# A hybrid decoder step on one core: projection pieces, output tiles and paired state products in the mixer's heads

## The chip, the cores and the metric

The kernel runs on one core of a Trainium2 chip. Its engines have their own instruction streams and meet at semaphores: TensorE (PE, with its weight loads shown apart as PEld), VectorE (DVE), ScalarE (ACT), GpSimd (POOL) and SyncE (SP), which issues most of the DMAs. The metric is the device time of one execution in microseconds (us). Three executions of the kernel before took 1274.74, 1276.26 and 1278.26 us, median 1276.26.

## The reference

One decoder layer in float32 for a prompt of 512 tokens and for 8 samples of 8 tokens each (64 rows, with a state from the past). Both go through a mixer and then through a mixture of 64 experts. This is the mixer, cut to what matters here:

```python
z = einsum('bld,de->ble', h, w_in)                 # one projection of 1024 to 4104 columns
# mLSTM heads (4), per chunk of 128 tokens (a sample is one chunk of 8)
s   = einsum('bihd,bjhd->bijh', q, k) * w_intra
num = einsum('bijh,bjhe->bihe', s, v) + w_inter * einsum('bihd,bhde->bihe', q, C)
C_new = w_old * C + einsum('bjh,bjhd,bjhe->bhde', w_k, k, v)
# retention heads (4): q and k rotated, fixed decays instead of gates
y = einsum('bhij,bjhe->bihe', scores, v) + inter * einsum('bihd,bhde->bihe', q, S)
S_new = exp(L * log_g) * S + einsum('jh,bjhd,bjhe->bhde', k_w, k, v)
out = concat([head_norm(h_m) * sigmoid(mo), head_norm(y_r) * silu(rg)])
x = x + gt1 * rms_norm(out @ w_out)                # then the experts
```

The states C and S are 128 x 128 for each head and each sample; the kernel keeps the mLSTM normaliser as a 129th column of C.

## The kernel before, in words

The instructions of each engine are written by hand in one order per engine; semaphores (`S["..."]`) tie them together, and no scheduler moves anything. Every float32 matmul of the program is two MATMUL records of the trace, each with a weight load; a transpose is one.

**Projection.** The 1024 x 4104 weights come in eight blocks of 512 columns (2 MB each) through a ring of two slots. The first blocks (mLSTM v, q, k) are multiplied in one go before the heads. The other five (`mo`, `rq`, `rk`, `rv`, `rg`) are cut into halves of a unit, each of 8 steps (one step is one matmul over 128 of the 1024 input channels; 128 x 288 out for a channel unit, up to 128 x 256 for an `rv` unit, whose halves are columns). Their 336 steps are the filling of the heads: `fill(filled(h, p))` on TensorE works off steps up to a count that a table gives for head h and phase p. The halves alternate between banks 6 and 7, and ScalarE copies them out (`evac_halves`).

**Heads.** Eight heads follow each other (h = 0 to 3 mLSTM, 4 to 7 retention). On TensorE a head is: `chunks(h)`, four chunks of 128 tokens, each with two or three products and, from chunk 1 on, a wait for `nchunk` (VectorE has added the state of the chunk before); the scores and the key transposes of head h+1 stand in chunks 1 and 2; a fill ends each chunk. Then `samples(h)`: one product inside the samples and eight with their states (`q8`, 64 columns of which 8 are not zero, one sample each, added up in bank 5). Then `out_T(h-1)`, the transposes of the normed head before; `head_a(h+1)`, which opens the next head and waits for `ynT_ready` (VectorE has gated those transposes); and `deltas(h)`: eight products of 64 key rows, masked to one sample (`kw8`), with the values, in three groups of banks. VectorE adds them to the states (`sdu` counts it), then makes the masked scores of the next head (`stm`), and `chunks(h+1)` waits for both.

VectorE also rotates rq and rk (`rotate`, eight pieces of four instructions) and does the head norm in two parts, `norm_a` (statistics) and `norm_b`.

**Loads.** SP runs its DMAs in order: the states of the retention heads (`stS`, 2 MB) go into ring slot 0 when `rv` is done; the first half of w_out (`woA`, 2 MB) into ring slot 1 when the last projection half is done. GpSimd's queue stores the states when the last head's `sdu` is complete, waits for that store, and then loads `bcB`, the modulation rows of the expert input, into the place of `stS`.

**After the heads.** `y_mm(t)` multiplies output tile t (128 tokens; tile 4 the 64 sample rows) by w_out: 16 matmuls of 128 x 512, two banks. `y_mm(t)` from t = 2 waits for `x1_done` of tile t-2. VectorE then makes the residual row (`x1_done`) and the expert input (`h2_ready`, needs `bcB`), one tile after the other.

Of the kernel before, what the change touches and what calls it, by code (L numbers as in the profile page):

```python
# [9 lines left out]
ALU = mybir.AluOpType  # L10
# [101 lines left out]
def build(nc, A, O, K):  # L112

    ctx = ExitStack()
    with ctx:
# [245 lines left out]
        HALVES = 2 * (NU - UM)  # L361
        PHASES = 7
        BEFORE = 2 * 2 * HS
        SHARE = [64, 64, 56, 56, 22, 21, 21, 0]
        assert BEFORE + sum(SHARE) == HALVES * HS

        def filled(h, p):

            return BEFORE + sum(SHARE[:h]) + SHARE[h] * (p + 1) // PHASES

        def units_done(u):

            return u if u <= UM else UM + 2 * (u - UM)
# [350 lines left out]
        def _(act):  # L724
# [87 lines left out]
            def evac_halves(steps):  # L812

                nonlocal evacuated
                while evacuated < steps // HS:
                    g = evacuated
                    u, hf = UM + g // 2, g % 2
                    kind, nm, bi, c = UNITS[u]
                    bank = ps[6 + hf]
# [4 lines left out]
                    if kind == "tok":  # L824
# [14 lines left out]
            def head_c(h):  # L839
# [15 lines left out]
                evac_halves(filled(h, 4))  # L855
# [9 lines left out]
            for h in range(2 * H):  # L865
                head_c(h)
                if h + 1 < 2 * H:
                    head_a(h + 1)
                evac_halves(filled(h, 6))
# [95 lines left out]
        def _(pe):  # L965
# [88 lines left out]
            def fill(steps):  # L1054

                nonlocal stepped
                while stepped < steps:
                    g, k = stepped // HS, stepped % HS
                    kind, nm, bi, c = UNITS[UM + g // 2]
                    hf, w, bank = g % 2, ring[:, bi % 2, :].rearrange("p (c f) -> p c f", c=KC), ps[6 + g % 2]  # L1060
# [3 lines left out]
                    if kind == "tok":  # L1064
# [8 lines left out]
                    stepped += 1  # L1073

            def chunks(h):
# [9 lines left out]
                for c in range(NCH):  # L1085
# [12 lines left out]
                    fill(filled(h, c))  # L1098

            def samples(h):  # L1100
# [10 lines left out]
                for b in range(NB):  # L1111
                    st = stC[:, b, h, 0:w] if h < H else stS[:, b, h - H, :]
                    i = mm(ps[5][0:NS, 0:w], q8[:, b, :], st, start=b == 0, stop=b == NB - 1)  # L1113
# [3 lines left out]
            def deltas(h):  # L1117
# [3 lines left out]
                for bk, b0, b1 in DGROUPS:  # L1121
                    if b0 == 6:
                        fill(filled(h, 6))
                        pe.wait_ge(S["sdu"], h * NB + 3)
                    for b in range(b0, b1):
                        mm(ps[bk][:, (b - b0) * (DH + 1):(b - b0) * (DH + 1) + w], kw8[:, b, :], vv[0:NS, NCH, h, 0:w],
                           start=True, stop=True).then_inc(S["sdb"], 1)
# [59 lines left out]
            for h in range(2 * H):  # L1187
# [5 lines left out]
                if h == H:  # L1193
# [8 lines left out]
            def wo(k):  # L1202
                return woA[:, k, :] if k < H else woB0[:, k - H, :] if k < H + H // 2 else woB1[:, k - H - H // 2, :]

            def y_mm(t, heads=range(2 * H)):

                n = ROWS[t]
                if t >= 2:
                    pe.wait_ge(S["x1_done"], t - 1)
                if t == NCH:  # L1210
                    for k in heads:
                        for hf in range(2):
                            i = mm(y_half(t, hf), yT(k)[:, t * P:t * P + n],
                                   wo(k)[:, hf * 512:(hf + 1) * 512], start=k == 0, stop=k == 2 * H - 1)
                else:
                    for hf in range(2):
                        for k in heads:
                            i = mm(y_half(t, hf), yT(k)[:, t * P:t * P + n],  # L1218
                                   wo(k)[:, hf * 512:(hf + 1) * 512], start=k == 0, stop=k == 2 * H - 1)
                if heads[-1] == 2 * H - 1:  # L1220
                    i.then_inc(S["y_mm"], 1)
# [942 lines left out]
```

## Time and profile before

| | us |
|---|---|
| median of 3 executions | 1276.26 |
| profiled execution, device time | 1274.83 |
| its span in the trace | 1272.2 |
| TensorE busy in the span | 1164.1 (92%) |
| granted TensorE clock, mean | 0.962 |

The heads run from 200.73 us (first chunk product) to 471.31 us (first output tile), the output tiles to 537 us, the experts from about 588 us to the end. A row of the timeline is a run of like instructions, with its start, its length from the first start to the last end, and in brackets the idle time ahead of it and the instruction whose end released it. "PEclk" is the granted TensorE clock as a share of full speed (2.4 GHz), averaged over a stretch; an instruction runs at full or at half.

### The profile page before, as it was taken

To read this page: it belongs to the slowest core of one execution; us is meant where nothing else is said; L and a number is where in the kernel's file an instruction comes from. 1 tells how busy PE (TensorE), PEld (TensorE's weight loads), DVE (VectorE), ACT (ScalarE), POOL (GpSimd) and SP (SyncE) were. 2 spreads that over 40 slices of the span, in tenths; PEclk is the share of its full clock that TensorE was granted. 3 is DMA by queue.
4 is the path that set the end of the run, shared out by engine and by line. 5 is a ranking of instruction groups with operands and counts; after the bars stand their busy time and mean duration, and the time that the engine had idled before them with its cause. 6 is when DMAs were issued, how large, how long until landed. Compare 5 with 4: busy or idle time off the path is not lost.

```text
span 1272.2 us, 17204 instructions
## 1 busy us (share of the span) xinstructions
PE 1164.1 (92%) x6487; PEld 615.8 (48%) x6487; DVE 467.8 (37%) x1275; ACT 239.0 (19%) x517; POOL 150.4 (12%) x180
## 2 busy tenths in 40 slices
PE   2899999998898979998999999999999999999795
PEld 0435777767676754475434443434344344343232
DVE  0203551335533453574223623232232232232147
ACT  2302322221212211320111111111111111111111
POOL 5100000000010010011110211111111111111100
PEclk7999999999898989999999999999999999999868
DMA  9989231230116026184879899999999999999796
GB/s 277 324 284 309 69 54 25 58 66 18 50 52 231 1 110 221 82 316 147 341 311 414 330 395 419 417 420 403 383 419 368 407 420 382 414 398 374 259 375 264
DMA packets 75270, 337.26 MB, mean 265 GB/s; under 512 B 12250, under 2 KB 21182, under 8 KB 46126
## 3 DMA queue, kind: packets, MB, share of 16 engines
q1 hardware_dynamic: 56398, 287.25, 60.1%
q0 software_dynamic: 18784, 48.85, 10.5%
q8 instruction: 53, 0.87, 0.3%
q14 instruction: 35, 0.29, 0.1%
HBM read 312.45 MB, written 37.24 MB: 275 GB/s over the span
## 4 chain that ended last, share of the span: by engine, by line
PE 82%; DMA 8%; DVE 6%; issue 2%; ACT 1%; SPq 1%; POOLq 0%; DVEq 0%; POOL 0%; ACTq 0%
PE bank L1373 26%; PE bank L1397 13%; PE bank L1069 9%; PE bank L1218 4%; DMA mem<-in_w_ada 3%; PE bank L1361 3%; PE bank L1153 3%; PE bank L1066 3%; PE bank L1160 3%; PE bank L1161 2%; PE bank L1476 2%; DMA mem<-in_w_exp_down 2%; DMA mem<-expert_out_rows 2%; PE bank L997 1%; PE bank L1113 1%
## 5 line engine op out<-in xcount | busy, mean ns | idle before, releaser
L1373 PE MATMUL bank<-mem 128*32 128x512 f32 (+2 forms) x1424 | 307.0, 596 | 3.9 <-issue 3.0
L1373 PEld LDWEIGHTS bank<-mem 128*32 128x32 f32 (+2 forms) x1424 | 101.2, 127 | 162.3 <-issue 160.8
L1397 PE MATMUL bank<-mem 128*32 128x512 f32 (+2 forms) x712 | 157.0, 596 | 2.3 <-DMA mem<-in_w_exp_down 1.3
L1985 DVE COPY mem<-bank 128x512 f32<-128x512 f32 x49 | 33.9, 692 | 306.9 <-PE bank L1361 306.9
L1373 PE MATMUL bank<-x_sb,mem 128*32 128x512 f32 (+2 forms) x480 | 141.4, 594 | 1.2 <-issue 1.2
L1069 PE MATMUL bank<-hT,mem 128*128 128x288 f32 x512 | 135.5, 416 | 1.0 <-ACT mem L793 1.0
L1069 PEld LDWEIGHTS bank<-hT,mem 128*128 128x128 f32 x512 | 96.3, 195 | 26.7 <-issue 2.4
L925 ACT ACTIVATE mem<-bank 128x256 f32<-128x256 f32 x48 | 18.5, 385 | 322.7 <-PE bank L1383 322.7
L1397 PEld LDWEIGHTS bank<-mem 128*32 128x32 f32 (+2 forms) x712 | 48.8, 126 | 58.9 <-issue 58.0
L1397 PE MATMUL bank<-hT,mem 128*32 128x512 f32 (+2 forms) x240 | 72.8, 596 | 0.8 <-ACT mem L925 0.8
L1373 PEld LDWEIGHTS bank<-x_sb,mem 128*32 128x32 f32 (+2 forms) x480 | 43.6, 127 | 59.8 <-issue 59.8
L678 POOL DMA_INDIRECT mem<-ffn_in_rows,idxg x34 | 35.2, 1034 | 295.4 <-DVE idxs L1981 255.4
L2000 DVE COPY hT<-bank 128x512 f32<-128x512 f32 x48 | 33.2, 692 | 86.9 <-PE bank L1397 86.8
L694 POOL DMA_INDIRECT expert_out_rows<-hT,idxs x48 | 48.6, 1013 | 108.0 <-DVE hT L2000 99.3
L1218 PE MATMUL bank<-mem 128*128 128x512 f32 x128 | 55.6, 594 | 1.0 <-DVE mem L1745 1.0
L931 ACT ACTIVATE hT<-bank 128x512 f32<-128x512 f32 x48 | 28.7, 597 | 143.2 <-PE bank L1397 143.2
L997 PE MATMUL bank<-mem 128*32 128x512 f32 x192 | 27.0, 675 | 20.4 <-DMA mem<-in_w_ada 20.4
L1476 PE MATMUL bank<-mem,c_ident 128*128 128x512 f32 (+1 forms) x72 | 40.8, 729 | 3.8 <-DMA mem<-expert_out_rows 3.8
L1943 DVE SCALAR_TENSOR_TENSOR mem<-mem,c_iota 128x160 bf16<-128x160 f32 (+3 forms) x77 | 43.9, 571 | 0.3 <-issue 0.3
L1160 PE MATMUL bank<-hT,mem 128*128 128x288 f32 x128 | 41.9, 409 | 0.0
L1161 PE MATMUL bank<-hT,mem 128*128 128x288 f32 x128 | 41.5, 406 | 0.0
L1153 PE MATMUL bank<-mem,hT 128*128 128x512 f32 (+1 forms) x80 | 37.0, 620 | 2.3 <-DVE cvbuf L1529 2.3
(378 smaller groups left out, 1388.4 us busy)
## 6 DMA issues: line engine op xcount, KB each, us to landing
mem<-in_w_exp_gate SPq DMA_DIRECT2D x48, 1024.0 KB, 12.0
mem<-in_w_exp_up SPq DMA_DIRECT2D x48, 1024.0 KB, 17.3
mem<-in_w_exp_down SPq DMA_DIRECT2D x48, 1024.0 KB, 16.9
mem<-in_w_ada SPq DMA_DIRECT2D x12, 2048.0 KB, 15.6
mem<-in_w_in SPq DMA_DIRECT2D x8, 2048.0 KB, 13.4
x_sb<-in_w_exp_gate SPq DMA_DIRECT2D x16, 1024.0 KB, 11.3
x_sb<-in_w_exp_up SPq DMA_DIRECT2D x16, 1024.0 KB, 17.7
hT<-in_w_exp_down SPq DMA_DIRECT2D x16, 1024.0 KB, 16.2
```

The source lines that it names most:

```text
L694: pool.indirect_dma_start(y_d[:, :], bass.IndirectOffsetOnAxis(idxs[:, q:q + 1], 0), yo[:, q % 2, :], None, bounds_check=T * TOPK - 1, oob ...
L997: x = mm(ps[ADA_BANK[g]][32 * j:32 * j + 32, :], cTs[:, 2 * k + cc, :], ADA_SLOT[i][:, cc, j * 512:(j + 1) * 512], start=k == 0 and cc == ...
L1066: i = mm(bank[0:n, 0:2 * DH], hT[:, k, c * P:c * P + n], w[:, k, 2 * DH * hf:2 * DH * (hf + 1)], start=k == 0, stop=k == KC - 1)
L1069: i = mm(bank[:, 0:TH], w[:, k, c * P:(c + 1) * P], hT[:, k, hf * TH:(hf + 1) * TH], start=k == 0, stop=k == KC - 1)
L1153: i = mm(A0[0:n, :], hT[:, k, c * P:c * P + n], w[:, k, :], start=k == 0, stop=k == KC - 1)
L1160: mm(A0[0:m, 0:TH], st, hT[:, k, 0:TH], start=k == 0, stop=k == KC - 1)
L1161: i = mm(A1[0:m, 0:TH], st, hT[:, k, TH:T], start=k == 0, stop=k == KC - 1)
L1218: i = mm(y_half(t, hf), yT(k)[:, t * P:t * P + n], wo(k)[:, hf * 512:(hf + 1) * 512], start=k == 0, stop=k == 2 * H - 1)
L1373: i = mm(bank[sl, :].rearrange("p (m f) -> p m f", m=2), xT[:, j % 2, c * BLK + sl.start:c * BLK + sl.stop], wview(r)[0][:, :, c, :], star ...
L1397: i = mm(ps[4 + hf][sl, :], hhT[:, k * BLK + sl.start:k * BLK + sl.stop], wview(r)[1][:, k, hf * 512:(hf + 1) * 512], start=k == 0, stop=k ...
L1476: i = mm(ps[2 * (o % 2) + hf][0:n, :], ident[0:n, 0:n], yhalf[0:n, q % NYH, k * D + hf * 512:k * D + (hf + 1) * 512], start=False, stop=k ...
L1943: return stt(pm, p.to_broadcast([P, NT, w]), off, iota[:, 0:w].unsqueeze(1).to_broadcast([P, NT, w]), ALU.add, ALU.is_equal)
```

## The change

1. **Pieces.** The last `rv` unit (the 64 sample rows) was two halves of 64 x 256, 8 steps each. It is now one piece: each step issues two matmuls that write rows 0-63 and 64-127 of one bank. 41 pieces (328 steps) in place of 42 halves (336).
2. **Phases.** A table sets the steps for each head and each of now eight phases. The new last phase stands at the end of `deltas(h)`, ahead of `chunks(h+1)`. The fill of phase 5 stands ahead of `head_a(h+1)`, not behind it.
3. **Output tiles.** After each chunk of head 7 a quarter of `y_mm(0)` over heads 0 to 3 is issued (one half of the columns, two heads). Behind head 7 stand the products of `y_mm(1)` over heads 0 to 3, in banks 6 and 7, and after the last `out_T` the rest of tiles 0 and 1.
4. **Pairs.** The eight state products of the samples take 32 columns each and go in pairs to rows 0-31 and 32-63 of bank 5. The eight `deltas` products take 32 key rows each, in pairs from partitions 0-31 and 32-63, into banks 4 and 5; retention heads have one group, mLSTM heads two.
5. **VectorE.** `rotate` is called at three places of a head, once with at most one piece after chunk 1 and once ahead of `samples`; in head 7 `norm_a` stands ahead of `deltas`.

```diff
-        SHARE = [64, 64, 56, 56, 22, 21, 21, 0]
+        PHASES = [[8, 8, 8, 8, 7, 7, 7, 7]] * 4 + [[3, 3, 3, 3, 0, 4, 0, 6], [3, 3, 2, 2, 0, 4, 0, 6], [2, 2, 1, 1, 0, 3, 0, 5], [0] * 8]
-        DGROUPS = [(4, 0, 3), (5, 3, 6), (4, 6, NB)]
+        def dgroups(h):
+            return [(0, HB - 1), (HB - 1, HB)] if h < H else [(0, HB)]
         def y_banks(t):
-            return (1, 2) if t % 2 == 0 else (0, 3)
+            return [(1, 2), (6, 7), (1, 2), (0, 3)][t]
...
@@ fill
+                    if hf == 2:
+                        for j in range(2):
+                            i = mm(bank[NS * j:NS * j + NS, 0:2 * DH], hT[:, k, SEQ:T], w[:, k, 2 * DH * j:2 * DH * (j + 1)],
+                                   start=k == 0, stop=k == KC - 1)
@@ chunks
                     fill(filled(h, c))
+                    if h == 2 * H - 1:
+                        if c == 0:
+                            pe.wait_ge(S["ld_woA"], 16)
+                        y_mm(0, range(H // 2 * (c % 2), H // 2 * (c % 2 + 1)), [c // 2])
@@ samples
-                for b in range(NB):
-                    i = mm(ps[5][0:NS, 0:w], q8[:, b, :], st, start=b == 0, stop=b == NB - 1)
+                for b in range(HB):
+                    for j in range(2):
+                        r = slice(HR * j, HR * j + HR)
+                        i = mm(ps[5][r, 0:w], q8[:, HB * j + b, r], st, start=b == 0, stop=b == HB - 1)
@@ deltas
+                    for i in range(i0, i1):
+                        for j in range(2):
+                            r = slice(HR * j, HR * j + HR)
+                            mm(ps[4 + j][:, dcols(h, i)], kw8[r, HB * j + i, :], vv[r, NCH, h, 0:w], start=True, stop=True).then_inc(S["sdb"], 1)
+                fill(filled(h, 7))
@@ the head loop of TensorE
+                fill(filled(h, 5))
                 if h + 1 < 2 * H:
                     head_a(h + 1)
-                fill(filled(h, 5))
                 deltas(h)
-            pe.wait_ge(S["ld_woA"], 16)
-            y_mm(0, range(H))
+            pe.wait_ge(S["proj_evac"], units_done(NU))
+            y_mm(1, range(H))
             out_T(2 * H - 1)
@@ the head loop of VectorE
+                rotate(filled(h, 0), 1)
                 chunk(h, 2)
...
                 if h + 1 < 2 * H:
                     masks(h + 1)
+                else:
+                    norm_a(h)
                 deltas(h)
```

On TensorE, the end of head 5 up to the first product of head 6 stood like this before (L1049 and L1050 are `head_a(6)`, L1126 `deltas(5)`, L1069 fill, L1088 chunk 0 of head 6):

```order
L1049 MATMUL bank<-mem 64x64 [waits ynT_ready]
L1050 MATMUL bank<-c_ident,mem 64x128
L1069 MATMUL bank<-hT,mem 128x288 x3
L1126 MATMUL bank<-mem 128x128 [waits s_nc]
L1126 MATMUL bank<-mem 128x128 x5
L1069 MATMUL bank<-hT,mem 128x288 [waits proj_evac,ld_w1]
L1069 MATMUL bank<-hT,mem 128x288 x2
L1126 MATMUL bank<-mem 128x128 [waits sdu]
L1126 MATMUL bank<-mem 128x128
L1088 MATMUL bank<-mem 128x128 [waits kwa,stm,sdu]
```

And so the same place of the changed kernel (L1088 is now fill, L1063 and L1064 `head_a(6)`, L1174 `deltas(5)`, L1128 chunk 0 of head 6):

```order
L1088 MATMUL bank<-hT,mem 128x288 [waits proj_evac,ld_w1]
L1088 MATMUL bank<-hT,mem 128x288 x3
L1063 MATMUL bank<-mem 64x64 [waits ynT_ready]
L1064 MATMUL bank<-c_ident,mem 64x128
L1174 MATMUL bank<-mem 128x128 [waits s_nc]
L1174 MATMUL bank<-mem 128x128 x7
L1088 MATMUL bank<-hT,mem 128x288 x4
L1088 MATMUL bank<-hT,mem 128x288 [waits proj_evac,ld_w1]
L1088 MATMUL bank<-hT,mem 128x288
L1128 MATMUL bank<-mem 128x128 [waits kwa,stm,sdu]
```

Four fill steps moved ahead of `head_a`, six stand between the last delta and the next head's first product, and the deltas are one block without a wait for `sdu` inside.

On TensorE, the first chunks of head 7, before:

```order
L1088 MATMUL bank<-mem 128x128 [waits kwa,stm,sdu]
L1089 MATMUL bank<-mem 128x128
L1088 MATMUL bank<-mem 128x128 [waits nchunk]
L1089 MATMUL bank<-mem 128x128
L1092 MATMUL bank<-mem 128x128
L1088 MATMUL bank<-mem 128x128 [waits nchunk]
```

and in the changed kernel (L1110 is `y_mm`):

```order
L1128 MATMUL bank<-mem 128x128 [waits kwa,stm,sdu]
L1129 MATMUL bank<-mem 128x128
L1110 MATMUL bank<-mem 128x512 [waits ld_woA]
L1110 MATMUL bank<-mem 128x512
L1128 MATMUL bank<-mem 128x128 [waits nchunk]
L1129 MATMUL bank<-mem 128x128
L1132 MATMUL bank<-mem 128x128
L1110 MATMUL bank<-mem 128x512 x2
L1128 MATMUL bank<-mem 128x128 [waits nchunk]
```

Two output matmuls stand behind each chunk, and the wait for `woA`, which stood behind head 7, stands behind its chunk 0.

## Rows read from the trace of the kernel before

**Rows 1.** Windows, TensorE: stretch and length, busy (count), PEclk, DMA share, GB/s.
```profile
200.73:377.53 176.80, 160.71 (x792) 0.97 0.18 38
377.53:454.46 76.93, 65.72 (x358) 0.93 0.34 115
454.46:467.85 13.39, 9.00 (x41) 0.63 0.36 144
467.85:529.16 61.31, 59.96 (x163) 1.00 0.49 170
```

**Rows 2.** TensorE's waits from 178 to 545 us: total, times, longest.
```profile
PE bank L1047 <- DVE mem L1745: 6.6, 2, 3.8
PE bank L1088 <- DVE x_sb L1701: 4.4, 3, 1.5
PE bank L1088 <- DVE mem L1701: 4.4, 3, 1.5
PE bank L1110 <- DMA mem<-in_state_ret_S: 3.7, 1, 3.7
```

**Rows 3.** Timeline of TensorE in head 1: start, length, instructions.
```profile
260.77 4.53 PE L1069 MATMUL bank<-hT,mem 128*128 128x288 f32 x18
...
265.59 1.97 PE L1113 MATMUL bank<-x_sb,mem 128*64 128x129 f32 x16
...
277.43 6.04 PE L1069 MATMUL bank<-hT,mem 128*128 128x288 f32 x18
283.40 1.60 PE L1126 MATMUL bank<-mem 64*128 64x129 f32 x12
...
289.98 0.71 PE L1126 MATMUL bank<-mem 64*128 64x129 f32 x4
```

**Rows 4.** Timeline of TensorE elsewhere: products that use part of the array, and whole ones.
```profile
44.64 0.42 PE L1017 MATMUL bank<-c_ident,mem 9*128 9x9 f32 x16 [1.53 <-DVE mem L1519]
44.91 0.65 PE L1022 MATMUL bank<-c_ident,mem 24*128 24x24 f32 x8
171.16 1.06 PE L1173 MATMUL bank<-woldr,c_sel 4*128 4x12 f32 x8
480.12 34.60 PE L1218 MATMUL bank<-mem 128*128 128x512 f32 x80 [1.04 <-DVE mem L1745]
530.13 7.09 PE L1213 MATMUL bank<-mem 128*64 128x512 f32 x32
```

**Rows 5.** Timeline of TensorE: a sample half of `rv`; chunk 3 of head 5.
```profile
366.18 3.67 PE L1066 MATMUL bank<-mem,hT 128*64 128x256 f32 x16
...
414.82 0.38 PE L1088 MATMUL bank<-mem 128*128 128x128 f32 x2
```

**Rows 6.** Timeline of VectorE: a rotation's last part, chunk 3 of head 5, head 7, first tiles.
```profile
270.73 0.76 DVE L1634 TENSOR_TENSOR mem<-mem,x_sb 128x576 f32<-128x576 f32 x1
...
416.37 0.34 DVE L1685 SCALAR_TENSOR_TENSOR mem<-mem,c_gL,bank 128x128 f32<-128x128 f32 x1
...
469.76 2.27 DVE L1701 SCALAR_TENSOR_TENSOR mem<-mem,c_gL,bank 128x128 f32<-128x128 f32 x8
471.94 1.05 DVE L1710 BATCH_NORM_STATS2 mem<-mem 128x6 f32<-128x128 f32 x5
...
473.50 0.25 DVE L1724 COPY hstat<-mem 128x5 f32<-128x5 f32 x1
...
501.29 1.28 DVE L1812 SCALAR_TENSOR_TENSOR mem<-x_sb,stat,mem 128x1024 f32<-128x1024 f32 x1 [7.40 <-DMA mem<-mod_rows]
...
506.58 1.23 DVE L1806 TENSOR_TENSOR x_sb<-x_sb,mem 128x1024 f32<-128x1024 f32 x1
```

**Rows 7.** Timeline of SP: when the two loads into the ring are issued.
```profile
375.01 6.83 SPq L498 DMA_DIRECT2D mem<-in_state_ret_S  x8
...
452.38 0.39 SPq L510 DMA_DIRECT2D mem<-in_w_out  x1
```

**Rows 8.** DMA issues from 440 to 475 us: `woA`, with us to landing.
```profile
mem<-in_w_out SPq DMA_DIRECT2D x1, 2048.0 KB, 7.6
```

More of the change, by code:

```diff
@@ L360, in build @@
         HS = KC
[L361 to L362 removed]
+        PIECES = [(u, hf) for u in range(UM, NU) for hf in ((2,) if UNITS[u][0] == "tok" and UNITS[u][3] == NCH else (0, 1))]
         BEFORE = 2 * 2 * HS
[L364 to L365 removed]
+        PHASES = [[8, 8, 8, 8, 7, 7, 7, 7]] * 4 + [[3, 3, 3, 3, 0, 4, 0, 6], [3, 3, 2, 2, 0, 4, 0, 6], [2, 2, 1, 1, 0, 3, 0, 5], [0] * 8]
+        assert BEFORE + sum(sum(p) for p in PHASES) == len(PIECES) * HS
         def filled(h, p):
[L369 removed]
+            return BEFORE + sum(sum(q) for q in PHASES[:h]) + sum(PHASES[h][:p + 1])
         def units_done(u):
[L373 removed]
+            return u if u <= UM else UM + sum(1 for v, _ in PIECES if v < u)
         def unit_banks(u):
@@ L1073, in fill, with wo, y_mm @@
                     stepped += 1
+            def wo(k):
+                return woA[:, k, :] if k < H else woB0[:, k - H, :] if k < H + H // 2 else woB1[:, k - H - H // 2, :]
+            def y_mm(t, heads=range(2 * H), halves=range(2)):
+                n = ROWS[t]
+                if t >= 2:
+                    pe.wait_ge(S["x1_done"], t - 1)
+                if t == NCH:
+                    for k in heads:
+                        for hf in range(2):
+                            i = mm(y_half(t, hf), yT(k)[:, t * P:t * P + n],
+                                   wo(k)[:, hf * 512:(hf + 1) * 512], start=k == 0, stop=k == 2 * H - 1)
+                else:
+                    for hf in halves:
+                        for k in heads:
+                            i = mm(y_half(t, hf), yT(k)[:, t * P:t * P + n],
+                                   wo(k)[:, hf * 512:(hf + 1) * 512], start=k == 0, stop=k == 2 * H - 1)
+                if heads[-1] == 2 * H - 1:
+                    i.then_inc(S["y_mm"], 1)
             def chunks(h):
@@ L1120, in deltas @@
                 pe.wait_ge(S["s_nc"], h + 1)
-                for bk, b0, b1 in DGROUPS:
-                    if b0 == 6:
+                for i0, i1 in dgroups(h):
+                    if i0:
                         fill(filled(h, 6))
[L1124 to L1127, printed above, removed]
+                        pe.wait_ge(S["sdu"], h * NB + 2 * i0)
+                    for i in range(i0, i1):
+                        for j in range(2):
+                            r = slice(HR * j, HR * j + HR)
+                            mm(ps[4 + j][:, dcols(h, i)], kw8[r, HB * j + i, :], vv[r, NCH, h, 0:w], start=True, stop=True).then_inc(S["sdb"], 1)
+                fill(filled(h, 7))
             def out_T(h):
@@ L1229, in _ @@
             y_mm(0, range(H, 2 * H))
+            y_mm(1, range(H, 2 * H))
             def h2_T(t):
@@ L1320, in positions @@
                 i.then_inc(S["pos_mm"], 1)
-            y_mm(1)
             for t in range(2, NT):
@@ L1618, in _, with rotate @@
             rotated = 0
-            def rotate(steps):
+            def rotate(steps, most=2 * H):
                 nonlocal rotated
-                first = UEND["rq"] - H - UM
-                while rotated < 2 * H and 2 * HS * (first + rotated + 1) <= steps:
+                first, most = UEND["rq"] - H - UM, rotated + most
+                while rotated < min(2 * H, most) and 2 * HS * (first + rotated + 1) <= steps:
                     i8 = rotated
@@ L1775, in _ @@
                     masks(h + 1)
+                else:
+                    norm_a(h)
                 deltas(h)
```

67 lines of the change are left out of this document (30 added, 37 removed).

## The prediction

> **What bounds the kernel now.** I read the table of stages first, then who waits for whom, then the timeline where they wait. TensorE is busy for 92% of the span, so the question is where it is not, and where it runs at half clock. The windows split the mixer into stages [rows 1]: heads 0 to 3 take 176.8 us, of which TensorE is busy 160.7; heads 4 to 6 take 76.9 with 65.7 busy; head 7 up to its state products 13.4 with 9.0 busy at a mean clock of 0.63; from there to the end of output tile 3 it is 61.3 with 60.0 busy. Idle are 16.1, 11.2, 4.4 and 1.3 us. The waits name the places [rows 2]: `head_a` on the gated transposes (L1047, 6.6 us in two waits), the first product of a head on the delta updates (L1088, 4.4 and again 4.4 us, 1.5 each), and in head 4 the product with the loaded state (L1110, 3.7 us). Where the reader sees an idle of some 3 us, the next block is longer for the same work: 18 projection matmuls take 6.04 us behind one and 4.53 otherwise [rows 3]. That is half clock. The means of 0.97, 0.93 and 0.63 [rows 1] say it lasts for up to 5.3, 5.4 and 5.0 us of lost time; part of that passed while TensorE stood idle, so I count 4.8 and 4.3 for the first two.
>
> TensorE is thus the bound in heads 0 to 3, where each chunk has 4 us of filling; in heads 5 to 7, with 0 to 3 steps a chunk, it is the loop of TensorE, ScalarE and VectorE from one chunk to the next: a chunk starts at 414.82 and VectorE's update ends at 416.71 [rows 5, 6], 1.9 us.
>
> **Part by part.** The sum is made against the profiled execution, 1274.83 us (span 1272.2 and 2.6 around it), 1.4 under the median.
>
> *Pairs, samples.* Eight products are 16 records in 1.9 us a head (1.97 with the last one's tail) [rows 3]. The trace has column pairs elsewhere: 80 whole products of 512 columns start every 0.43 us (34.60 over 80), 32 of 64 columns in alternation start every 0.22 [rows 4]. Two side by side cost what one does. So 0.95 a head is saved; bounds 0 and 0.95.
>
> *Pairs, deltas.* 16 records take 1.53 and 0.65, some 2.2 us [rows 3]. The trace has no full product on row groups. The nearest rows are short transposes: 16 from four row groups start in 0.27 us, 0.017 apart, where 8 from one start 0.06 apart [rows 4]. So row groups work beside each other, and I take half, 1.1 a head. The other end is that their weight loads queue: 8 products with 128-column weights and 12 moving columns start 0.115 apart in one row group (1.06 less a 0.25 tail, over 7) [rows 4], so 16 need 1.8 us and 0.35 is saved. Together the pairs give 2.04 a head.
>
> For those loads the Trainium skill, "TensorE: Matmul & The Clock Gate", section "LDWEIGHTS (loading the stationary operand)", has a rule against this part: a load costs by its columns (columns / 1.2 ns), not by its rows. An estimate from that page is 107 ns for each of the 16, 1.7 us a head, if none lies beside another; its Part 3, "The mechanism", says loads do overlap when the row group differs. By the first the pairs of deltas would give 0.5 a head and the sum would be 1238, by the second it stays. The 0.017 us between transposes speaks for the second; no run here shows it for full products.
>
> *Pieces.* A sample half of `rv` takes 3.6 us [rows 5]; two become one of the same length. 8 steps go, 3.6 us. They go from heads 4 to 6 (64 steps to 56); heads 0 to 3 keep 240. At 0.243 us a record (4.53 less a 0.41 tail, over 17) [rows 3] a step is 0.49, 3.9 in all.
>
> *Phases in heads 0 to 3.* Behind the last delta stand 7 steps, 3.4 us. VectorE needs there two updates and the masked scores, about 1.5 us; the waits of 1.5 go, with 1.9 us of slack. `head_a` gets 7 steps ahead of it, so the gated transposes have 3.4 us for their 1.0 us. A rotation costs four instructions of 0.76 [rows 6], 3.05 us. Before, up to two stood ahead of the gating; now one does, and from chunk 3 it gets done some 2 us before TensorE asks. Two still stand at the end of head 1: they hold the copies of head 2's chunk 0 for 8 us, TensorE has 3.4 + 0.4 + 3.9 of work, 0.8 remains. ScalarE's copies out of banks 6 and 7 come after its exponentials; the tightest has 1.5 us to spare. So: 176.8 - 16.1 idle + 0.8 - 4.8 clock - 4 x 2.04 + 0.4 = 148.9, 27.9 less (the 0.4: eight of the 240 steps are now channel steps of 0.49, not `rv` steps of 0.44).
>
> *Heads 4 to 6.* `stS` is issued when `rv` is done, 375.01 [rows 7], and landed for L1110 16 us later, sharing the queues with the store of the other states. `rv` is done at the same count (264) and 13.8 us of work now stand behind it, so 2.2 us of the 3.7 stay, with 1.5 of clock. The first product of each head still waits 0.5, 0.5 and 1.0: 8 updates take 2.27 [rows 6] plus 0.9 of scores against 6, 6 and 5 steps (2.9, 2.9, 2.4). The wait on `n_out` (1.1) stays. With only 2 and 1 steps behind chunks 2 and 3, the 1.9 us loop is late by 0.3 in head 5 and 1.8 in head 6, and `out_T`, now right behind the state products, waits 0.35 twice for the masked keys. Left are 8.5 of idle. 76.9 - 2.7 idle - 2.8 clock - 3 x 2.04 - 3.9 = 61.4, 15.5 less.
>
> *Head 7.* Here the change adds a wait. `woA` may be issued only when the last projection piece has freed its ring slot: before at 452.38, 2 us ahead of head 7, with 7.6 us to landing [rows 7, 8], covered by the whole of head 7. Now that piece is the last instruction ahead of head 7, VectorE lets chunk 0 start about 1.0 us after it, and the first output quarter stands behind chunk 0. TensorE then waits from 0.4 to 6.65 us after the head's start, and chunks 1 to 3, VectorE's chain and all behind them wait with it. Then the four quarters, 16 records of 0.43: 7.0. The rest of the head's work is at full clock about 4.3 (9.0 busy at 0.63, less the pair's 0.95). The 6 us of idle bring half clock; behind the shorter ones it cost 1.5 and more [rows 3], I take 2.5. 6.65 + 7.0 + 4.3 + 2.5 = 20.4 in place of 13.4: 7.0 more.
>
> *Output tiles.* The 7.06 us of tile 1's first half stand where tile 0's stood, and cover the norm of head 7 as before; 16 records fewer are behind. But VectorE's order moves: `norm_a`, from 471.94 to 473.75, now stands ahead of the updates that ended at 472.03 [rows 6]. So the last `sdu`, on which GpSimd's queue waits with the store of the states and behind it the loads of `bcB`, comes 1.8 later after the state products. VectorE's first tile waited for `bcB` until 501.29, 29.3 us after `sdu`, and gave tile 1's residual at 507.8 [rows 6], 6.5 later. `y_mm(3)` needs that: behind the state products it has 2.0 (transposes, deltas) + 7.06 + 0.8 + 1.0 + 14.1 + 14.1 + 0.9 = 40.0 us of work ahead of it, and may start 6.0 + 29.3 + 6.5 = 41.8 after them. With its 13.8 it ends at 55.6, before 61.3: 5.7 less, not 7.1. From there on nothing moves against each other.
>
> Sum: -27.9 - 15.5 + 7.0 - 5.7 = -42.1; 1274.83 - 42.1 = 1232.7, told as 1233 us. The experts start earlier by the same amount, and their loads, which wait for the same tiles, with them.
>
> **The rivals.**
> 1. *Row groups load one after another.* Deltas save 0.35, not 1.1: 8 x 0.75 = 6.0 lost, 1239; if column pairs give nothing either, 7.6 more, 1246. For: no full product on row groups in the trace; against: the transposes.
> 2. *The heads are paced by VectorE and ScalarE.* Less work on TensorE then only makes its waits longer: the 16.1 and the clock of heads 0 to 3 stay. 1233 + 15.3 + 4.8 = 1253. For: all the waits there end on VectorE [rows 2]. Against: waits of 1.5 us against 3.4 of filling put in front of them. The same time comes out if the fillers only move the waits, from the head's end to the chunks (`nchunk`): the change then doesn't do what it says.
> 3. *Pairs empty the array, and it is slower.* If TensorE drains between two instructions on different groups, each of the 256 records of the pairs takes its whole latency, about 0.27 us (1.60 over 12 started 0.12 apart [rows 3] leaves 0.27 for the last), 69 us in place of 16: 1233 + 53 = 1286. It decides from 0.23 us a record on. Against it stand the 64-column products at 0.22 for 512 columns, half of the whole ones.
> 4. *`woA` lands late.* Nothing else is loaded then; if it took twice as long, 7.6 more: 1241. In the range, not a case of its own.
>
> **How the numbers follow.** Forecast 0.66, by itself 1224 to 1242: below, if head 7's clock and the waits of heads 4 to 6 fall away (2.5 + 6); above, if `woA` is late or the slacks of 1.5 to 2 us in heads 0 to 3 are not there. Rival 1 0.15, rival 2 0.14, rival 3 0.03, other 0.02. The range 1222 to 1252 leaves the slow case, half of what lies around rival 2 and a tail below outside. A measurement of this kernel tells about 0.3% (3.8 us) from no change. Faster by more than that: forecast, rivals 1 and 2, 0.95; slower 0.03; the same 0.02.
>
> **What would show it.** In the new profile: heads 0 to 3 in about 149 us at a clock of 1.00, with no wait over 1 us; the state products of a head in 1.0 us, the deltas in 1.1 (1.8 by rival 1, over 4 each by rival 3); a wait of about 6 us on the w_out load in head 7 and half clock behind it; a wait of some 2 us of `y_mm(3)` for tile 1's residual. The prediction is wrong if heads 0 to 3 stay above 160 us, if the w_out wait is missing or above 10, or if the experts' stretch changes its length.

## The result: 1235.8 us after 1275.5, and the profile of the changed kernel

The changed kernel takes 1235.8 us (median of 4 runs, 1233.2 to 1241.8), the kernel before beside it 1275.5. The ratio is 0.9693, with a 95% interval of 0.9654 to 0.9732. The forecast was 1233 with a range of 1222 to 1252. The profiled execution after has a span of 1233.9 us against 1272.2, 38.3 less.

The windows of TensorE in the changed kernel, cut at the same instructions as [rows 1], and a fifth from the end of output tile 3 to the first product of the experts (stretch and length, busy, granted clock, DMA share, GB/s):

```profile
203.48:354.94 151.46, 151.17 (x808) 0.99 0.21 47
354.94:414.89 59.95, 53.81 (x342) 0.97 0.38 138
414.89:434.91 20.02, 13.04 (x56) 0.83 0.29 106
434.91:489.97 55.06, 52.17 (x148) 1.00 0.53 180
489.97:550.08 60.11, 55.05 (x309) 0.97 0.53 202
```

| stage | before | predicted | after |
|---|---|---|---|
| heads 0 to 3 | 176.8 | 148.9 | 151.5 |
| heads 4 to 6 | 76.9 | 61.4 | 60.0 |
| head 7 to its state products | 13.4 | 20.4 | 20.0 |
| from there to the end of output tile 3 | 61.3 | 55.6 | 55.1 |

The four stages give 41.9 us; 42.1 were forecast. Outside them heads 0 to 3 begin 2.75 us later (203.48 against 200.73). That lies ahead of all that the change touches, and it is this execution alone: in all the other profiles the heads begin between 200.3 and 201.7. The stretch to the experts is 60.1 us, before 58.5, at a clock of 0.97 against 1.00. The rest is 683.8 us against 684.5, unchanged.

In heads 0 to 3 TensorE is now idle for 0.29 us in 151. The waits of TensorE from 178 to 510 us (in total, times, longest) answer to [rows 2]:

```profile
PE bank L1110 <- DMA mem<-in_w_out: 6.9, 1, 6.9
PE bank L1154 <- DMA mem<-in_state_ret_S: 2.9, 1, 2.9
...
PE bank L1110 <- DVE x_sb L1838: 1.8, 1, 1.8
...
```

The waits of `head_a` on the gating (6.6 us) and of the heads' first products on the state updates (4.4 and 4.4) are not in the list any more. The longest wait of the mixer is the new one, on W_out.

### The profile page after: what moved, and what is told of

It reads as the page before. It is cut to its first block, busy times and chain, and to the rows that moved or that the text cites. A ratio compares the mean times of both kernels' runs of the same rounds, so it can differ in the third digit from the quotient of the medians.

```text
span 1233.9 us, 17204 instructions
## 1 busy us (share of the span) xinstructions
PE 1138.2 (92%) x6487; PEld 592.0 (48%) x6487; DVE 465.7 (38%) x1275; ACT 241.7 (20%) x519; POOL 150.4 (12%) x180
## 4 chain that ended last, share of the span: by engine, by line
PE 79%; DMA 12%; DVE 5%; issue 2%; SPq 0%; ACT 0%; POOL 0%; POOLq 0%; DVEq 0%; ACTq 0%
PE bank L1402 26%; PE bank L1426 14%; PE bank L1088 9%; PE bank L1390 3%; PE bank L1201 3%; DMA mem<-in_w_in 3%; PE bank L1208 3%; PE bank L1209 3%; PE bank L1505 2%; PE bank L1085 2%; DMA mem<-in_w_ada 2%; DMA mem<-in_w_exp_down 2%; PE bank L1110 2%; DMA mem<-expert_out_rows 2%; PE bank L1011 1%
## 5 line engine op out<-in xcount | busy, mean ns | idle before, releaser
L1088 PE MATMUL bank<-hT,mem 128*128 128x288 f32 x512 | 134.8, 414 | 2.0 <-DVE n_out L1804 1.0
L1088 PEld LDWEIGHTS bank<-hT,mem 128*128 128x128 f32 x512 | 95.0, 192 | 27.8 <-issue 2.4
L1110 PE MATMUL bank<-mem 128*128 128x512 f32 x128 | 58.2, 609 | 9.8 <-DMA mem<-in_w_out 6.9
L1110 PEld LDWEIGHTS bank<-mem 128*128 128x128 f32 x128 | 24.3, 194 | 38.3 <-issue 27.8
L1208 PE MATMUL bank<-hT,mem 128*128 128x288 f32 x128 | 41.9, 409 | 0.0
```

The lines of the kernel that those rows point to most:

```text
L1088: i = mm(bank[:, 0:TH], w[:, k, c * P:(c + 1) * P], hT[:, k, hf * TH:(hf + 1) * TH], start=k == 0, stop=k == KC - 1)
L1110: i = mm(y_half(t, hf), yT(k)[:, t * P:t * P + n], wo(k)[:, hf * 512:(hf + 1) * 512], start=k == 0, stop=k == 2 * H - 1)
L1208: mm(A0[0:m, 0:TH], st, hT[:, k, 0:TH], start=k == 0, stop=k == KC - 1)
```

## The experiments

Each kernel was timed beside the kernel before on the same chip. Where the changed kernel ran beside it too, the difference to it is given in us; otherwise it follows from the ratios (the changed kernel has 0.9693, and twice more 0.9690 and 0.9669). The interval of one ratio is 2 to 4 us to either side, so a difference of two kernels is known to some 4 us. Where that does not decide, the waits in the profiles do.

**The changed kernel again**, with its two repetitions: 1235.0 us, ratio 0.9690 (0.9667 to 0.9712), and 1232.5, 0.9669 (0.9644 to 0.9693).

> The changed kernel once more, as the reference for what runs beside it, and to see which of its stretches recur. If the missing 2.6 us of heads 0 to 3 (151.5 against 148.9 forecast) come from the structure, the 5.35 us stretch of 14 projection matmuls behind the first deltas of head 0 (3.66 us in the other heads) is there again; if it is a chance of the clock, it is elsewhere or gone, and heads 0 to 3 take about 149.5 us. The late start of the heads (203.5 against 200.7 us) is a matter of the first weight loads and should vary. Time 1233 to 1239 us; the wait on the w_out load in head 7 again 6 to 7.5 us.

> The changed kernel once more, as the reference on the chip of the next two: 1232 to 1238 us, ratio 0.966 to 0.971.

Heads 0 to 3 take 151.5 us in both again. The stretch at half clock that costs them 1.7 us is not behind head 0's first deltas but behind head 2's: 4.98 us for 14 records in both, where 3.29 is the length at full clock. It recurs, at another place. The wait on W_out is 7.2 and 7.1 us.

**Without the pairs.** Both kinds of sample products over the full width, all else as changed:

```
-  for b in range(HB):
-      for j in range(2):
-          r = slice(HR * j, HR * j + HR)
-          i = mm(ps[5][r, 0:w], q8[:, HB * j + b, r], st, ...)
+  for b in range(NB):
+      i = mm(ps[5][0:NS, 0:w], q8[:, b, :], st, ...)
...
-  r = slice(HR * j, HR * j + HR)        (deltas)
+  r = slice(0, NS)
```

> Both kinds of pairs undone: the samples' state products are 8 products of 64 columns again, the deltas use all 64 key rows; all else as in the changed kernel. Theory (pairs run side by side and TensorE sets the pace): a head's state products take 1.9 us in place of 1.0, its deltas 2.1 in place of 1.1 to 1.3, so 0.9 + 0.9 us a head, 8 heads: 14.5 us more, about 1250. Rival (VectorE and ScalarE set the pace of the heads, TensorE's shorter work only makes it wait longer): below 4 us more, 1236 to 1240.

Measured: 1243.9 us, 8.8 above the changed kernel, between the two theories. The products themselves behave as theory A says. Timeline of TensorE in head 5 without pairs, then of the changed kernel again (start, length, instruction):

```profile
392.40 1.96 PE L1157 MATMUL bank<-mem 128*64 128x128 f32 x16
...
397.71 2.05 PE L1172 MATMUL bank<-mem 64*128 64x128 f32 x16
```
```profile
388.05 1.07 PE L1159 MATMUL bank<-mem 128*32 128x128 f32 x16
...
392.55 1.16 PE L1174 MATMUL bank<-mem 32*128 32x128 f32 x16
```

That is 0.9 us each, 1.78 a head, 14.2 in eight heads. Read against the profile of the changed kernel's repetition, the rest comes back at three places: the load of the later heads' states is waited for 1.9 us, not 2.6; the first pieces behind that wait take 2.2 us, not 4.2 (half clock); and a piece behind head 2's first deltas takes 3.3, not 5.0 (half clock too, the last section). Head 7 then starts 7.7 us later, not 12.5. Only 0.7 us of this is the load. The 3.7 us of clock stand in one profile of each kernel, and that the pairs bring them is not shown.

**The pairs in another order**: the same narrow products, but the eight of the first group and then the eight of the second.

```
-  for b in range(HB):
-      for j in range(2):
+  for j in range(2):
+      for b in range(HB):
```

> Same products as the changed kernel, in another order: the 8 of the first column (row) group and then the 8 of the second, where the changed kernel alternates. Theory A (the gain of the pairs is that neighbours on different groups run side by side): 16 state products take 1.9 to 2.0 us again and 16 delta products 2.0 to 2.3, as where they used the whole width (1.97 and 2.05 to 2.31), and the time is that of the kernel without pairs, 8 to 9 us above the changed kernel. Theory B (a product on a quarter or half of the array is cheaper by itself, in any order): 1.1 and 1.2 to 1.4 us as in the changed kernel, and no difference in time (under 1.5 us).

Measured: ratio 0.9720 (0.9707 to 0.9734), 3 to 7 us above the changed kernel. Head 5 of it:

```profile
388.58 1.53 PE L1159 MATMUL bank<-mem 128*32 128x128 f32 x16
...
393.46 1.71 PE L1174 MATMUL bank<-mem 32*128 32x128 f32 x16
```

The 16 records lie between the two theories: 1.53 between 1.07 and 1.96, 1.71 between 1.16 and 2.05. The starts of the single records say why. These are the deltas of head 5 that have started by 1.0 us after the first of them, without pairs and then in this order (the count is the last number; in the changed kernel again all 16 have):

```profile
397.71 1.27 PE L1172 MATMUL bank<-mem 64*128 64x128 f32 x9
```
```profile
393.46 1.26 PE L1174 MATMUL bank<-mem 32*128 32x128 f32 x12
```

Without pairs the records start 0.112 us apart. In this order the starts make two series of eight, each again 0.112 apart, and the second begins at 394.01, while the first has three to go (394.12 to 394.34). Read as the two groups, they run side by side for a part of the time even in this order, and a narrower product gains nothing by itself. Theory A has the mechanism right; the order does not take all of it away. The state products do the same: 0.109 us apart over the full width, and 0.109 in each of two series here.

For the load of 128 columns the Trainium skill ("TensorE: Matmul & The Clock Gate", section "LDWEIGHTS (loading the stationary operand)") gives columns / 1.2 ns whatever the rows, an estimate of 0.107 us from that page; the trace agrees within a series (0.112). Its Part 3 says that loads on different row groups overlap; the trace agrees (neighbours of a pair start 0.007 us apart). Whether the load or the 128 columns that are moved through set it here is open, since either does alone: 128-column loads with 12 moving columns start 0.115 apart [rows 4], and state products with 32 columns loaded and 128 moving 0.109.

**The pieces where they were**: counts spread evenly, none behind the last delta, the fifth phase behind the gate rows.

```
-  PHASES = [[8, 8, 8, 8, 7, 7, 7, 7]] * 4 + [[3, 3, 3, 3, 0, 4, 0, 6], ...]
+  PHASES = [[8, 9, 8, 9, 8, 9, 9, 0]] * 4 + [[3, 3, 3, 3, 3, 7, 0, 0], ...]
...
-  fill(filled(h, 5))
   if h + 1 < 2 * H:
       head_a(h + 1)
+  fill(filled(h, 5))
...
```

> The steps spread over the phases as before the change: none behind the last delta of a head, the fill of phase 5 behind head_a; the number of steps of each head, pairs and tiles as in the changed kernel. Theory (the new places cover waits on VectorE): heads 0 to 3 wait again for updates and scores (1.5 to 1.9 us a head), for the gated transposes (1 us in three heads) and for the two rotations (2 us), heads 4 to 6 about 3.4 us at each end and 1 for the gated transposes; some 20 us and 3 to 5 us of half clock, less about 4.5 us because the last projection piece, and with it the w_out load, is ready earlier ahead of head 7: 15 to 21 us more, about 1253. Rival (the steps only move the waits from one place to another): within 4 us of the changed kernel.

Measured: 1250.7 us, 15.6 above the changed kernel, as the theory says. Its waits of TensorE, 178 to 515 us:

```profile
PE bank L1128 <- DVE mem L1731: 9.4, 3, 3.1
PE bank L1128 <- DVE x_sb L1731: 4.5, 3, 1.5
PE bank L1063 <- DVE mem L1775: 3.1, 3, 1.0
PE bank L1110 <- DMA mem<-in_w_out: 2.6, 1, 2.6
PE bank L1061 <- DVE mem L1775: 2.1, 2, 1.0
```

The waits of [rows 2] are back: on the state updates (L1731) 13.9 us in six heads, on the gating (L1775) 5.2. But W_out is waited for 2.6 us in place of 6.9 to 7.2, and the states of heads 4 to 7 no longer. The last piece now stands ahead of head 6's deltas, so SP issues the load of W_out 4.2 us ahead of head 7 (429.35 against 433.54) and not 0.5; and the waits that are back give both loads time. This hides some 7 us of what the step is worth.

**The gate rows first**, one part of that by itself: only the order of `fill(filled(h, 5))` and `head_a(h + 1)` is put back.

> One step undone, the counts of the pieces unchanged: the pieces that stand between the state products and the next head's gate rows (7 steps in heads 0 to 3, 3 to 4 in heads 4 to 6) go behind the gate rows again. Theory A (these pieces hide VectorE's gating of the transposed output, of which the gate rows need the bank): TensorE waits 1.04 us for it in heads 1 to 6, as it does where the old counts were put back, 6.2 us in all, and each of these comes back in full since the pieces behind hide nothing of their own: 5.5 to 7 us slower than the changed kernel. Theory B (the wait only moves time, because VectorE's state updates begin by so much later and the first product of the next head is then early): 0 to 2 us slower.

Measured: 1240.1 us, 7.5 above the changed kernel beside it; theory A. Its waits:

```profile
PE bank L1063 <- DVE mem L1775: 3.1, 3, 1.0
...
PE bank L1061 <- DVE mem L1775: 2.1, 2, 1.0
```

These are 5.2 us; one of the head starts is covered by the wait on `n_out`, which stands at the same place. Each wait comes back in full, although every other count is as changed.

**The sample rows of `rv` in two pieces again**, the 8 steps more in heads 4 to 6.

```
-  PIECES = [(u, hf) for u in range(UM, NU) for hf in ((2,) if ... else (0, 1))]
+  PIECES = [(u, hf) for u in range(UM, NU) for hf in (0, 1)]
```

> One part undone: the sample rows of the rv projection are again two pieces of 8 steps on the whole width, in place of one on two column groups; the 8 steps more are spread over heads 4 to 6. Theory A, the prediction's term (8 steps of 0.49 us, 3.6 to 3.9 us, on TensorE's path): 3.6 to 3.9 us slower than the changed kernel. Theory B: rv is now done at step 272, the last before head 4, not at 264, so the load of the states of heads 4 to 7, which waits for it, is issued 3.9 us later against head 4's first product and TensorE waits 5.5 to 7 us for it, not 2.6 to 2.9; with it head 4 also waits some 0.5 us for the copy of rv's last piece: 7 to 9 us slower.

Measured: 1240.7 us, 8.1 above the changed kernel (the spans of the two profiles differ by 4.6); theory B by its waits, which have

```profile
PE bank L1110 <- DMA mem<-in_w_out: 7.8, 1, 7.8
PE bank L1154 <- DMA mem<-in_state_ret_S: 5.7, 1, 5.7
```

so the wait for the states is 3.3 us longer (2.4 in the changed kernel beside it) and that for W_out 0.7 (7.1). The 8 steps are 3.9 us of work, but they do not come on top: heads 5 and 6, where 7 of them stand, begin at 381.83 and 400.59 and end at 418.32, and in the changed kernel at 379.42, 397.63 and 414.87. Each is 0.5 us longer. The steps fill waits on VectorE's chunks (L1714), 1.6 us in the changed kernel and 0.2 here. Heads 4 to 6 are 4.3 us longer in all, and 3.3 of that is the states' load: most of what the merged piece is worth there is that `rv` ends 8 steps sooner and its load leaves sooner.

**Head 7 without output tiles**: tile 0's first half behind the heads, tile 1 whole behind tile 0.

```
-  if h == 2 * H - 1:
-      if c == 0:
-          pe.wait_ge(S["ld_woA"], 16)
-      y_mm(0, range(H // 2 * (c % 2), H // 2 * (c % 2 + 1)), [c // 2])
...
```

> The output tiles taken out of head 7: the first half of tile 0 stands behind head 7 as before the change, tile 1 whole behind tile 0; pairs and phases as in the changed kernel. Theory (the early wait on the w_out load eats what the tiles fill): head 7 up to its state products takes about 12 us in place of 20.0, from there to the end of tile 3 it is 60.6 in place of 55.1: 2.5 us less, about 1233. Rival (the tiles fill waits, as their place says): the 7.06 us of matmuls come back behind the head, 1240 to 1243.

Measured: 1232.3 us, ratio 0.9671 (0.9651 to 0.9690), 2.7 below the changed kernel. The intervals of the two ratios overlap, so this part of the change costs a little or nothing. In its head 7 the waits are short ones:

```profile
413.99 0.49 PE L1128 MATMUL bank<-mem 128*128 128x128 f32 x2 [1.16 <-DVE mem L1711]
...
416.97 0.80 PE L1128 MATMUL bank<-mem 128*128 128x128 f32 x2 [1.64 <-DVE mem L1711]
```

and come to 5 us, where the changed kernel waits 6.9 us for W_out and 0.5 beside it. Here, too, half clock follows: the state products of head 7 take 1.92 us and not 1.07.

**Head 7 filled from rows that have landed**: in the four gaps heads 4 and 5 of tiles 0 and 1, whose W_out rows land in head 4; tile 0's heads 0 to 3 behind head 7.

```
-  if c == 0:
-      pe.wait_ge(S["ld_woA"], 16)
-  y_mm(0, range(H // 2 * (c % 2), H // 2 * (c % 2 + 1)), [c // 2])
+  if c == 0:
+      pe.wait_ge(S["ld_woB"], 32)
+  if c == 2:
+      pe.wait_ge(S["proj_evac"], units_done(NU))
+  y_mm(c // 2, range(H, H + H // 2), [c % 2])
...
```

> Head 7's filling no longer takes W_out rows 0-3, which land last: its four pieces are now heads 4 and 5 of output tiles 0 and 1 (rows that landed before head 5 began), and heads 0-3 of tile 0 come behind head 7. The number of products is the same. Theory A (the 6.9 to 7.2 us wait for the load is on the path, and the first piece behind it runs at half clock, 3.65 against 1.88 us): the wait and the slow piece go, 7.2 + 1.8 = 9.0 us, less up to 1 us of waits of TensorE on VectorE in head 7 that the long wait covered, and less up to 1.5 us because output tile 3's wait on VectorE (1.4 to 1.8 us) grows when TensorE is earlier and the mod rows are not: 6.5 to 9 us faster than the changed kernel, ratio 0.962 to 0.964 against the kernel before. Theory B (the wait hides another one: the DMA of the mod rows or VectorE's last deltas end the stretch anyway): the time is given back at output tile 3, 0 to 3 us faster.

Measured: 1224.1 us, ratio 0.9609 (0.9587 to 0.9631): 7.6 to 10.7 us below the changed kernel, theory A. Chunk 0 and the first piece of its head 7, then the changed kernel's:

```profile
410.36 0.46 PE L1128 MATMUL bank<-mem 128*128 128x128 f32 x2 [0.50 <-issue]
...
410.88 1.88 PE L1110 MATMUL bank<-mem 128*128 128x512 f32 x4
```
```profile
414.89 0.46 PE L1128 MATMUL bank<-mem 128*128 128x128 f32 x2 [0.50 <-issue]
...
422.51 3.65 PE L1110 MATMUL bank<-mem 128*128 128x512 f32 x4 [6.93 <-DMA mem<-in_w_out]
426.66 1.88 PE L1110 MATMUL bank<-mem 128*128 128x512 f32 x4
```

The wait goes, and the 1.8 us of half clock behind it. From head 7's start to the end of output tile 3 it is 65.9 us (410.36 to 476.29), where the changed kernel takes 75.1 (414.89 to 489.97).

**Head 7's statistics behind the state updates**, as before the change.

```
-  else:
-      norm_a(h)
   deltas(h)
...
+  norm_a(2 * H - 1)
   norm_b(2 * H - 1)
```

> One part undone: VectorE does head 7's statistics behind its last state updates, as before the change, not ahead of them. Theory A (the state updates free the place of the mod rows, whose load ends what output tile 3 waits for): the updates end 1.7 us earlier (statistics 1.05 + 0.44 + 0.17), so does the load, and the wait of 1.4 to 1.8 us of output tile 3 on tile 1's residual sum goes: 1.4 to 1.8 us faster than the changed kernel. Against it: head 7's normed rows come 1.7 to 2.1 us later; they have 7.1 us of the products of heads 0-3 of tile 1 in front of their transposes, and the transposes begin within 0.3 us of the end of these, so up to 2 us could come in there: Theory B, no difference (under 0.5 us).

Measured: ratio 0.9672 (0.9646 to 0.9699), 0 to 3 us below the changed kernel: by the time alone inconclusive. The profile shows the mechanism: output tile 3 waits 0.3 us for tile 1's residual.

```profile
471.02 14.00 PE L1110 MATMUL bank<-mem 128*128 128x512 f32 x32 [0.29 <-DVE x_sb L1837]
```

**Both together**: the edits of the last two kernels.

> Both at once: head 7 filled from W_out rows that have landed, and VectorE's last statistics behind the state updates. If the two are separate terms (theory A of both) their gains add: 8 to 10.5 us faster than the changed kernel, about 1225 to 1227 us. If output tile 3's wait on the mod rows takes back part of the first alone, this one is the faster by more than the sum of the two alone. If one wait hides the other (theory B), it is as fast as the better of the two alone.

Measured: 1220.0 us (1218.9 to 1225.3), ratio 0.9588 (0.9568 to 0.9607): the fastest of all, 10 to 13 us under the changed kernel and 53 under the kernel before. Output tile 3 has no wait left, and from head 7's start to the end of tile 3 it takes 64.6 us (409.97 to 474.57) against 75.1:

```profile
432.26 27.73 PE L1110 MATMUL bank<-mem 128*128 128x512 f32 x64 [1.03 <-DVE mem L1777]
459.84 1.04 PE L995 MATMUL bank<-c_ident,mem 128*128 128x128 f32 x8
460.73 14.00 PE L1110 MATMUL bank<-mem 128*128 128x512 f32 x32
```

**Three parts undone at once**: full-width products, `rv` in two pieces, and the steps spread evenly as in the kernel before.

```
-  PHASES = [[8, 8, 8, 8, 7, 7, 7, 7]] * 4 + [[3, 3, 3, 3, 0, 4, 0, 6], ...]
+  PHASES = [[s * (p + 1) // 7 - s * p // 7 for p in range(7)] + [0] for s in (64, 64, 56, 56, 22, 21, 21, 0)]
...
```

> The three large parts undone together: counts and places of the pieces as before (spread evenly over the phases, none behind the last delta, the fifth behind the gate rows), samples' products and deltas over the full width, the sample rows of rv as two pieces. Left of the change are the output tiles in head 7, the rotations one at a time, the deltas in two groups and head 7's statistics. Undone one at a time the three cost 15.6, 8.8 and 8.1 us. Theory A (they add, and what is missing to the kernel before comes from the small parts left): 32.5 us above the changed kernel, 1265 to 1269 us, ratio 0.992 to 0.996. Theory B (they cover for each other: with the pairs and the pieces in place each hides a part of what another loses): more than the sum, 1272 to 1278 us, ratio 0.998 to 1.002, and the small parts give nothing together. Theory C (they overlap: the time that one loses lies in waits that another makes anyway): less than the sum, under 1262 us.

Measured: 1274.2 us, ratio 0.9994 (0.9979 to 1.0010). All that the change gives is gone, 38 to 41 us by the ratios. The time is that of theory B, since one by one the three cost 15.6 + 8.8 + 8.1 = 32.5 us. That they cover for each other is not shown by it, though: each of the three differences is known to some 4 us, and the steps do not stand as in the kernel with only the pieces moved back. Heads 0 to 3 have 64, 64, 56 and 56 of them and not 60 each, and in heads 4 to 6 the last three or four stand behind the last delta, because a retention head has one group of deltas. The waits:

```profile
PE bank L1110 <- DMA mem<-in_w_out: 6.3, 1, 6.3
PE bank L1128 <- DVE mem L1706: 5.3, 1, 5.3
PE bank L1154 <- DMA mem<-in_state_ret_S: 5.0, 1, 5.0
```

The last steps and the first product of head 7 here, then the last deltas and the first product of head 7 with only the pieces moved back:

```profile
448.27 1.72 PE L1088 MATMUL bank<-hT,mem 128*128 128x288 f32 x6
451.43 0.46 PE L1128 MATMUL bank<-mem 128*128 128x128 f32 x2 [1.43 <-DVE mem L1729]
```
```profile
429.25 1.16 PE L1174 MATMUL bank<-mem 32*128 32x128 f32 x16
433.54 0.77 PE L1128 MATMUL bank<-mem 128*128 128x128 f32 x2 [3.13 <-DVE mem L1731]
```

The states are waited for (5.0 us, none with only the pieces moved back), since with two `rv` pieces their load leaves last. W_out is waited for 6.3 us and not 2.6, since the last steps stand behind head 6's deltas: SP issues the load at 450.02, 1.4 us ahead of head 7, and not 4.2. The wait of 5.3 us (L1706) is in chunk 1 of head 2, behind three rotations; with only the pieces moved back it is 2.1 us behind two, in the changed kernel 0.3. So a part of the 6 to 9 us by which the three together exceed the sum is the other table, and how large a part stays open. What is left of the change here (output tiles in head 7, rotations one at a time, deltas in two groups, statistics first) gives nothing that shows: between 2.7 us faster and 1.3 slower than the kernel before.

## Why the prediction was right, step by step

*Pairs, samples* (0.95 a head) came as priced: the 16 records of [rows 3] now take 1.07.

*Pairs, deltas* (1.1 a head) were mis-sized. In head 0 of the changed kernel:

```profile
223.24 1.07 PE L1159 MATMUL bank<-x_sb,mem 128*32 128x129 f32 x16
...
233.02 0.94 PE L1174 MATMUL bank<-mem 32*128 32x129 f32 x12
233.89 5.35 PE L1088 MATMUL bank<-hT,mem 128*128 128x288 f32 x14
239.17 0.49 PE L1174 MATMUL bank<-mem 32*128 32x129 f32 x4
```

0.94 and 0.49 make 1.43 where 1.1 was taken; the saving is 0.9. The group of four carries the latency of its last product, which I counted once and not twice. Over heads 0 to 3 that is 1.3 us of the 2.6 by which the stage was missed; 1.7 is the 7 steps (14 records) at 5.35 us between them, which take 3.66 in head 1. Rival 1 (loads that queue) put the deltas at 1.8 a head; they are well below. One group's starts do queue as it says (0.112 us apart); two groups do not queue behind each other (0.007).

*Pieces* (8 steps, 3.9): the kernel with `rv` whole lost 8.1, but hardly by the steps. Put back, they fill waits on VectorE and lengthen heads 4 to 6 by about 1.0 us, where 3.9 was taken; the states' load gives 3.3. One statement was false: that `rv` is done at the same count. It was done at the last step before head 4 and is now done 8 steps sooner. What I gave the load's earlier issue (a wait of 3.7 down to 2.2) was put down to the moved phases; the experiment shows that the piece's merging gives it. The wait that is left is 2.9.

*Phases in heads 0 to 3*: the waits went, and what I named as late next came at its place, head 2's chunk 1, with 0.29 us and not 0.8; my own terms (8 us against 3.4 + 0.4 + 3.9) leave 0.3. The gate-rows experiment shows one of the mechanisms alone: 5.2 us of waits. The spans of its profile and of the changed kernel's beside it differ by 5.9; what makes the medians differ by 7.5 is not placed. Rival 2 (VectorE and ScalarE pace the heads) is refuted by TensorE's 151.2 busy of 151.5.

*Heads 4 to 6*: 6.1 us idle against 8.5 reckoned, less what half clock behind the states' wait takes back (16 records 1.92 us and not 1.07), so 60.0 and not 61.4.

*Head 7*: wait 6.9 (6.65), half clock in the first quarter only, total 20.0 (20.4). SP issued the load at 414.42, 0.5 ahead of the head, with 8.0 us to landing; before it was 2 us ahead with the whole head as cover [rows 7, 8]. The kernel with other rows in the gaps shows that this wait is on the path: without it the stretch to tile 3's end is 9.2 us shorter.

*Output tiles*: 55.1 (55.6). VectorE in the changed kernel, the last state updates and the first tiles, answering to [rows 6], and TensorE's wait:

```profile
438.30 2.15 DVE L1731 SCALAR_TENSOR_TENSOR mem<-mem,c_gL,bank 128x128 f32<-128x128 f32 x8
...
469.56 1.28 DVE L1844 SCALAR_TENSOR_TENSOR mem<-x_sb,stat,mem 128x1024 f32<-128x1024 f32 x1 [10.05 <-DMA mem<-mod_rows]
...
474.85 1.23 DVE L1838 TENSOR_TENSOR x_sb<-x_sb,mem 128x1024 f32<-128x1024 f32 x1
```
```profile
476.13 14.00 PE L1110 MATMUL bank<-mem 128*128 128x512 f32 x32 [1.79 <-DVE x_sb L1838]
```

The load of the mod rows lands 29.1 us after the last update (440.45 to 469.56; 29.3 was taken from before), and tile 3 waits 1.8 us (2 foretold). With the statistics behind the updates the wait is 0.3.

Rival 3 (pairs drain the array) is refuted by 1.07 us. Rival 4 (the load of W_out takes twice as long) did not come: in the changed kernel's three profiles it takes 8.0 to 8.3 us and the wait is 6.9 to 7.2.

Two readings of the sum are to be corrected. It came out right because it walked through the new order once; its terms are not the worth of the parts. The merged piece was worth a load more than its steps, and the pieces put back alone cost some 7 us less than they would if both loads had stayed as late. And that the four stages agree to 0.2 us is luck, by errors of both signs: heads 0 to 3 too low by 2.6, heads 4 to 6 too high by 1.5, head 7 and the tiles too high by 0.9. The start (2.75 us, this execution alone) and the stretch to the experts (1.6) stood in no term.

## What to carry to other kernels

Filling moved into a gap is worth the gap only if its operands are there: ask for each piece which load it needs and when that may be issued. Here the tiles placed at the gaps cost up to 2.7 us with the rows that land last, and the same number of products from rows that had landed gave 8 to 11. When a step makes a stretch shorter, look for the loads issued at its start: they are waited for next. Undoing one part alone can then show less than the part is worth (7 us were hidden for the pieces), or show a load's worth in place of its own (the merged piece).

## What the runs showed of the chip that was not expected

Narrow products gain by their neighbours and not by being narrow. Records of deltas start 0.112 us apart on 64 rows, and 0.112 apart in each series on 32 rows; with the groups alternating, neighbours start 0.007 us apart. 16 of them took 2.05 us on 64 rows and 1.16 with the groups alternating. With one group after the other they took 1.71, since the second series began while the first had three to go.

TensorE's granted clock fell to its lower level (1.2 GHz) with no idle before it. In the changed kernel it is the 7 steps at 233.89, right behind head 0's first deltas (granted clock 0.68 over their 5.35 us, 1.00 before and behind): TensorE had been busy without a gap since the head began. A block of 7 steps (14 records) beside the first deltas of one head took 5.0 to 5.4 us, not 3.3 to 3.7, in 7 of the 11 profiles with narrow products, in head 0, 1 or 2. In six of them it stands behind these deltas; With the gate rows first it stands ahead of them, shortly behind a wait of 1.0 us, and in two heads. In the three profiles with full-height products (the kernel before, without pairs, three parts undone) the clock fell in the heads only behind waits of 1.4 us or more. Whether the narrow products cause it was not tried; with one profile of each kernel, and 1.7 us a time, it stays open.

The same wait was followed by half clock in one execution and not in another. Behind 2.8 us for the states of heads 4 to 7 the pairs took 1.92 us in the fastest kernel (granted clock 0.50), and behind 2.8 us 1.53, their length at full clock, where the pairs stand in the other order (1.00). The stretch to the experts lost its 1.6 us in this way: behind the same idle of 2.5 us the first 16 records take 5.53 us in the changed kernel (0.74) and 4.12 in the kernel before (1.00).
